# A two-direction recurrence on one core: the inverse's second direction on off-diagonal quarters of the array, work banks in two pairs, the state's update ahead of the transposes

## The reference, cut to what matters

```python
def step(S, inp):
    r_t, w_t, k_t, v_t, kk_t, a_t = inp
    sa = jnp.einsum('bhvk,bhk->bhv', S, -kk_t)
    S = (S * w_t[:, :, None, :] + sa[..., None] * (kk_t * a_t)[:, :, None, :]
         + v_t[..., None] * k_t[:, :, None, :])
    return S, jnp.einsum('bhvk,bhk->bhv', S, r_t)
S, ys = lax.scan(step, S0, xs, reverse=reverse)      # once forward, once in reverse
```

## Time and profile before

| | us |
|---|---|
| median of 3 runs | 2581.54 |
| lowest and highest | 2580.11, 2587.41 |
| the profiled execution | 2585.16 |
| its span in the trace | 2583.6 |
| granted clock of PE, mean | 0.941 of full |

### The profile page before, as it was taken

One profiled execution on the slowest core, in us unless ns is written; L12 is line 12 of the kernel. 1 busy time (PEld: TensorE's weight loads), 2 busy tenths in 40 slices (PEclk: granted clock), 3 DMA queues, 4 the chain that ended last, 5 costly groups with the idle time before them and its releaser, 6 DMA issues. The chain is left out here.

```text
span 2583.6 us, 60917 instructions
## 1 busy us (share of the span) xinstructions
PE 2260.9 (88%) x26659; PEld 1830.6 (71%) x26659; DVE 1146.9 (44%) x1601; ACT 799.4 (31%) x1329; POOL 451.9 (17%) x335
## 2 busy tenths in 40 slices
PE   5899994788888998869799999999696778899998
PEld 3677782677777777757688888888563436688887
DVE  4633322666776667532422222222386652433333
ACT  2223322344334433221522112211433331542231
POOL 0222312644555446300000000000120000000000
PEclk8799896899999999989899999999798989999999
DMA  9566652000000000031122212121110002233332
GB/s 307 173 209 185 192 179 70 23 24 10 30 30 24 30 10 10 10 140 47 49 65 65 72 51 65 57 75 37 44 50 0 0 0 82 73 100 95 98 103 85
DMA packets 261822, 191.73 MB, mean 74 GB/s; under 512 B 11610, under 2 KB 252132, under 8 KB 261092
## 3 DMA queue, kind: packets, MB, share of 16 engines
q1 hardware_dynamic: 261604, 188.45, 24.0%
HBM read 170.60 MB, written 17.83 MB: 73 GB/s over the span
## 5 line engine op out<-in xcount | busy, mean ns | idle before, releaser
L486 DVE TENSOR_TENSOR ffn_lo<-ffn_raw,ffn_hi 128x1024 fp32r<-128x1024 f32 (+1 forms) x120 | 159.8, 1332 | 571.4 <-ACT ffn_hi L481 571.4
L493 PE MATMUL bank<-operand_hi,ffn_hi 128*128 128x512 f32 (+1 forms) x1056 | 378.9, 359 | 24.6 <-DVE operand_lo L455 24.4
L494 PE MATMUL bank<-operand_lo,ffn_hi 128*128 128x512 f32 (+1 forms) x1056 | 378.1, 358 | 0.0
L495 PE MATMUL bank<-operand_hi,ffn_lo 128*128 128x512 f32 (+1 forms) x1056 | 375.0, 355 | 0.0
L481 ACT CAST ffn_hi<-ffn_raw 128x1024 fp32r<-128x1024 f32 (+1 forms) x120 | 136.4, 1137 | 531.3 <-PE bank L495 531.1
L1569 POOL TENSOR_TENSOR lvl<-sc_b,level_mask 128x512 f32<-128x512 f32 x144 | 192.9, 1354 | 320.4 <-PE bank L1158 297.5
L493 PEld LDWEIGHTS bank<-operand_hi,ffn_hi 128*128 128x128 f32 x1056 | 200.4, 190 | 61.8 <-issue 22.4
L495 PEld LDWEIGHTS bank<-operand_hi,ffn_lo 128*128 128x128 f32 x1056 | 200.2, 190 | 29.9
L494 PEld LDWEIGHTS bank<-operand_lo,ffn_hi 128*128 128x128 f32 x1056 | 200.7, 190 | 27.2
L494 PE MATMUL bank<-ffn_g_lo,ffn_hi 128*128 128x512 f32 (+1 forms) x528 | 188.0, 356 | 0.0
L493 PE MATMUL bank<-ffn_g_hi,ffn_hi 128*128 128x512 f32 (+1 forms) x528 | 187.4, 355 | 0.0
(11 more groups left out here) (244 smaller groups left out, 4519.3 us busy)
## 6 DMA issues: line engine op xcount, KB each, us to landing
mod_raw<-in_mod_w SPq DMA_DIRECT2D x96, 512.0 KB, 6.1
ffn_raw<-in_ff_w SPq DMA_DIRECT2D x88, 512.0 KB, 3.9
ffn_raw<-in_ff_w SPq DMA_DIRECT2D x32, 704.0 KB, 4.5
proj_raw<-in_rw_wr SPq DMA_DIRECT2D x8, 512.0 KB, 4.5
proj_raw<-in_rw_wk SPq DMA_DIRECT2D x8, 512.0 KB, 4.6
proj_raw<-in_rw_wv SPq DMA_DIRECT2D x8, 512.0 KB, 4.9
rwkv_out_raw<-in_rw_wo SPq DMA_DIRECT2D x8, 512.0 KB, 4.3
qk_w_raw<-in_at_wq SPq DMA_DIRECT2D x8, 512.0 KB, 3.8
```

The costliest lines, as they stand in the source:

```text
L486: signal(eng, eng.tensor_tensor(self.lo[s][:, 0:k_tiles, :], self.raw[s][:, 0:k_tiles, :], self.hi[s][:, 0:k_tiles, :].bitcast(F32), ALU.s ...
L493: pe.matmul(out, w[0], x[0], start=first, stop=False)
L494: pe.matmul(out, w[0], x[1], start=False, stop=False)
L495: return pe.matmul(out, w[1], x[0], start=False, stop=last)
```

## The change

- T and Y (now L1163, L1173, L1176): the backward direction goes to the two off-diagonal quarters. T writes it to the other half of the partitions in a second bank; Y reads it back. For this Y needs the backward inverses with their halves exchanged, so ACT makes `inverse_swapped` after level 0 and after the additions of levels 1 to 4: two copies of 64x256 each (`swap`, L1498).
- The eight matrices are ordered direction first in `inverse`, `lvl` and `t_sb`; the cut on POOL walks the scores accordingly.
- PSUM: banks 4 to 7 become two pairs of 1024 columns. Every use (scores, turned keys, values, T, Y, side products) takes one of the two pairs in turn. Two-piece side products become one piece of 768 columns, turned keys are copied in one piece of 1024.
- The early parts leave Y and stand in the chain's own blocks: values for y within `u`, for the right-hand side within `rhs`, for the state within `sy`.
- DVE: a new call `flip` holds the transposes. It stands behind `sy`, so the state's update comes after Y's addition and ahead of the transpose.
- `PLACES` has fewer and partly moved entries (the second map moves from place 3 to 4, the third stays at 6, the fourth is at 8, the norm's product at 9).

```diff
@@ schedule
-                y(B, 2, following(0))
+                if B:
+                    y(B, 2)
                 extra(1)
                 if C:
-                    E.sy(C, 0)
+                    E.sy(C, 0, following(0))
+                flip(B, 2)
@@ TensorE
...
+                            elif kind == "score":
+                                pe.wait_ge(masked, 4 * rest[0] + 2 * rest[1] + 2)
...
                     def t(self, G, n):
...
-                        for w in range(2 * GROUP):
-                            for h in range(2):
-                                mm = pe.matmul(bank[half(h), w * CH:w * CH + CH], lvl[G.parity][n % 2][half(h), w, :],
-                                               inv_t[G.parity][half(h), w, :], start=True, stop=True)
+                        for q in range(GROUP):
+                            for e in range(2):
+                                w, out = GROUP * e + q, slice(512 * e + q * CH, 512 * e + q * CH + CH)
+                                for h in range(2):
+                                    mm = pe.matmul(bank[half(h ^ e), out], lvl[G.parity][n % 2][half(h), w, :],
+                                                   inv_t[G.parity][half(h), w, :], start=True, stop=True)
...
+                    def y(self, G, n):
+                        bank = self.work_free("y", G.g, n)
+                        pe.wait_ge(t_copied, self.use.of("t", G.g, n) + 1)
+                        pe.wait_ge(x_swapped, self.use.of("x", G.g, n - 1) + 1)
...
@@ VectorE
-                    def y(self, G, n, _):
+                    def y(self, G, n):
...
-                        if n < LEVELS - 1:
-                            dve.wait_ge(x_added, no + 1)
-                            self.turn_inverse(G)
...
+                    def flip(self, G, n):
+                        dve.wait_ge(x_added, self.use.of("y", G.g, n) + 1)
+                        self.turn_inverse(G)
@@ ScalarE
+                    def swap(self, G, n):
+
+                        for h in range(2):
+                            ins = a.copy(inv_s[G.parity][half(1 - h)], inv[G.third][half(h), GROUP:2 * GROUP, :])
+                        ins.then_inc(x_swapped, 1)
+
+                    def level0(self, G):
+                        act.wait_ge(level0_done, G.g + 1)
+                        self.swap(G, 0)
+
+                    def y(self, G, n):
+                        if n < LEVELS - 1:
+                            act.wait_ge(x_added, self.use.of("y", G.g, n) + 1)
+                            self.swap(G, n)
...
@@ backbone
-        c.bank = [ctx.enter_context(nc.psum_tensor(f"bank{n}", [P, 512], F32)) for n in range(8)]
+        c.bank = [ctx.enter_context(nc.psum_tensor(f"bank{n}", [P, 512], F32)) for n in range(4)]
+        c.pair = [ctx.enter_context(nc.psum_tensor(f"bank_pair{n}", [P, 1024], F32)) for n in range(2)]
+        c.bank += [c.pair[n // 2][:, 512 * (n % 2):512 * (n % 2) + 512] for n in range(4)]
```

More of the change, by code:

```diff
@@ L873, in score @@
             def score(G, i):
-                use.take("bank", "score", G.g, i)
+                use.take("work", "score", G.g, i)
                 E.score(G, i)
             def turn_keys(G):
-                use.take("bank", "keys", G.g), use.take("turn", "keys", G.g)
-                use.take("copy", "b", G.g), use.take("copy", "k", G.g)
+                use.take("work", "keys", G.g), use.take("turn", "keys", G.g)
                 E.turn_keys(G)
@@ L883, in turn_values @@
                 if G.j < 2:
-                    use.take("bank", "values", G.g), use.take("turn", "values", G.g), use.take("copy", "v", G.g)
+                    use.take("work", "values", G.g), use.take("turn", "values", G.g)
                     E.turn_values(G)
@@ L1028, in nothing @@
                 pass
[L1030 to L1035 removed]
+            diag = score = turn_keys = turn_values = level0 = cut = t = y = flip = early = rhs = u = sy = feature = readout = nothing
         with nc.Block() as block:
@@ L1168, in y @@
                             for h in range(2):
-                                mm = pe.matmul(bank[half(h), w * CH:w * CH + CH], t_sb[G.parity][half(h), w, :],
-                                               inv[G.third][half(h), w, :], start=True, stop=True)
-                            if step and w < 6:
-                                self.early_part(*step, w)
-                        mm.then_inc(x_ready, 1)
-                    def early(self, G, q):
-                        self.early_waits(G, q)
-                        for part in range(6):
-                            self.early_part(G, q, part)
@@ L1184, in early_waits, with early, chain_ready @@
+                        mm.then_inc(x_ready, 1)
+                    def early(self, G):
+                        self.chain_ready(G, 0)
+                        for e in range(2):
+                            self.rhs_values(G, 0, e)
+                        for e in range(2):
+                            self.state_values(G, 0, e)
+                    def chain_ready(self, G, q):
+                        need(pe, s_done, G.step(q) - 1)
                         if q == 0:
                             pe.wait_ge(masked, 4 * G.g + 4)
-                            pe.wait_ge(tok_copied, self.use.of("copy", "k", G.g) + 1)
+                            pe.wait_ge(tok_copied, self.use.of("turn", "keys", G.g) + 1)
@@ L1208, in y_values, with rhs_values @@
-                    def y_values(self, G, q, e, done):
+                                pe.wait_ge(tok_copied, self.use.of("turn", "values", G.g) + 1)
+                    def rhs_values(self, G, q, e):
+                        n = G.chunk(q, e)
+                        for h in range(2):
+                            pe.matmul(CHAIN[G.step(q) % 2][half(h), e * CH:e * CH + CH], sc_k[G.third][half(1 - h), q, e, 0, :],
+                                      vtok[G.pair][half(1 - h), n, :], start=(e == 0), stop=False, skip_group_check=True)
@@ new lines, in state_values @@
+                    def state_values(self, G, q, e):
+                        n = G.chunk(q, e)
+                        for h in range(2):
+                            mm = pe.matmul(CHAIN[G.step(q) % 2][half(h), 256 + e * CH:256 + e * CH + CH],
+                                           tok[G.third][half(1 - h), 1, 2 * q + e, :], vtok[G.pair][half(1 - h), n, :],
+                                           start=False, stop=False, skip_group_check=True)
+                        if e == 1:
+                            mm.then_inc(rhs_ready if G.j == q == 0 else early_done, 1)
@@ L1209, in y_values @@
+                    def y_values(self, G, q, e):
                         n = G.chunk(q, e)
@@ L1466, in turn_keys @@
                         need(act, y_ready, GROUP * (G.g - 2))
-                        for i, bank in enumerate((B_BANK, K_BANK)):
-                            a.copy(tok[G.third][:, i], bank[:].rearrange("p (n t) -> p n t", t=CH)).then_inc(tok_copied, 1)
+                        a.copy(tok[G.third][:].rearrange("p i n t -> p (i n t)"), work(self.use, "keys", G.g)[:]).then_inc(tok_copied, 1)
                     def turn_values(self, G):
```

361 lines of the change are left out of this document (178 added, 183 removed).

## The result

The changed kernel takes 2603.09 us (median of 6 runs, 2599.36 to 2617.67), the kernel before 2584.48 in the same comparison: ratio 1.0084, 95% interval [1.0057, 1.0111]. It is slower by 19 us, where 46 us less were forecast.

A forecast was written before the change was run, and what follows sets the result against it. PE was taken as full but not alone on the path, with waits in the chain's loop. Slots -32, last six slots -16, opening slots -3 and clock +5 gave -46 us: 2536 forecast, own range 2505 to 2565, overall 2490 to 2587.

The forecast's parts named there:

- I cost them at nothing: Early parts moved from Y into rhs, u and sy: no cost; 0.23 us per block if their cover failed.
- +1.9 us: Readout slot: the exchange ahead of the square delays step 1's product from 831.7 to 833.6 us.
- 0.74 us each: Exchange on ACT: two copies of 64x256, 120 times, 89 us more ACT time; bounds 0.37 and 1.18 us each.
- rival 2: Whole kernel slower because ACT's queue becomes the chain: 2536 + 71 = 2607 us, chance 0.13.
- I take what is counted above: Two PSUM pairs: only waits already counted, chiefly the fourth map; bounds 0 and 1.2 us per side use.
- Rival 3: The two pairs and their emptying eat the gain: 80 side uses wait 0.5 us each, 2576 to 2580, chance 0.12.
- The state's place: Late step on DVE: the state runs at 3.28 to 3.72 us, since it no longer waits for the transpose.
- late step: Chain step without side work: 5.45 us falls to about 3.9, and a run of such steps settles at about 4.1.
- +5 us: Clock term in the sum: a longer gap in the readout slot adds 0.8 us for six readout slots.
- Rival 4: Lower clock as PE's busy share falls to about 0.75: a quarter of steps slow gives +48, 2584 us; chance 0.08.
- T and Y on four quarters: T and Y blocks on PE each save 0.465 us of issue, 112 us over 240 blocks.

The follow-up runs named there:

- e17: e13 without the exchange and its waits, and with the transposes ahead of the state's update again: 2606.39 us, ratio 1.0083.
- e20: e17 with the early parts back inside Y, between its blocks: 2607.1 us, ratio 1.0084.
- e3: Changed kernel with next-step values moved from rhs to u in a pair's first step and the exchange of levels 2 to 4 behind sy: 2579.19 us, ratio 0.9978.
- e21: e2 with the early parts back inside Y, as before the change: 2588.0 us, ratio 1.0008.
- e1: Changed kernel, but in a pair's first step u and no longer rhs prepares the next step: 2596.22 us, ratio 1.0054.
- e7: Kernel before, with only the new wait of PE for the previous pair's last state in a pair's first step: 2597.31 us, ratio 1.0036.
- e2: Changed kernel with ACT's exchange of levels 2 to 4 behind sy, no longer directly behind u: 2584.79 us, ratio 1.0016.
- e4: Changed kernel with no exchange; Y's second direction reads the inverse as it lies, so that part of the result is wrong: 2582.27 us, ratio 1.0001.
- e18: e3 with the transposes ahead of the state's update on DVE, as before the change: 2587.19 us, ratio 1.0013.
- e6: Kernel before with only the state's update moved ahead of the transposes on DVE: 2584.69 us, ratio 0.999.
- e5: Changed kernel with T and Y on the diagonal quarters again, the exchange made but not used: 2618.56 us, ratio 1.0124.
- e13: e3 with T and Y on the diagonal quarters again: 2597.10 us, ratio 1.0065.

## Why the prediction was wrong

46 us less were forecast and 19 more came, 65 apart. The terms that failed are the two pairs with their pieces (shown, some 20 us), the exchange's place in ACT's queue (shown, 18), the early parts' wait (shown, 7 to 12) and the clock (+5 in the sum; 36 to 60 by an estimate, not shown by a run). In order of the prediction:

- **"I cost them at nothing"** (early parts) is the step that failed first. I looked at their issue, which is indeed free or better (e17 against e20, e3 against e21). I did not look at the wait that they bring: `chain_ready` asks for the previous pair's last state, and in the lone `rhs` it stands ahead of the scores and of everything else on PE. Before, it stood in Y(2), behind them. 7 us in the change (e1), 9 to 12 alone (e7).
- **The readout slot, "+1.9 us"** for the square. The mechanism was right, the exchange ahead of the square behind a late addition. But the addition itself was taken from the old trace at 830.71; it moves with the scores that now come 3 us later. The first step of six readout slots went from 7 to 14 us, where +1.9 was forecast.
- **The exchange, "0.74 us each"**: measured 0.82 a pair of copies. As time on ACT it costs next to nothing (e2 against e4, 2.5 us, within the noise). As a waiting instruction at the head of a queue it costs 18 us (e2). This was rival 2's mechanism, which I gave 0.13 and priced at 71.
- **Two pairs, "I take what is counted above"**: 1.2 us a pair's fourth map and about nothing for the rest; measured about 20 us (e20, e17). Rival 3 named the pairs and gave them 40 us; the new waits for a free pair are 10 us in e20's two rows, and whether the pairs, the pieces or their places cost the rest is not shown. "Not shown by any row" was the warning in my own text.
- **The state's place** was the source of half the gain in the late step, and it holds there (4.16 us; with four quarters but the transposes first, e18, the same steps take 4.9 to 5.9). In the whole kernel it gives 0 (e6) to 8 us (e18).
- **The clock, "+5 us"**: mis-sized. Rival 4 put PE's busy share at 0.75; measured 492/646 = 0.76, which is near for a lucky reason, as both parts were off: 435 busy in 576 us were forecast. PE was busy for longer than forecast in part because the same instructions take longer at half clock (1.55 to 2.92 us above). A fifth of the stretch then ran at half clock, close to rival 4's quarter, for which I had worked out +48. By 0.3 to 0.5 us per us, 119 us more at half clock are an estimate of 36 to 60 us. I treated it as a rival of its own, with 0.08, when it follows from the forecast: whoever takes 47 us of work from PE and none from the waits lowers its share.
- **T and Y on four quarters, 112 us of issue**: the block is as forecast (0.69 for 0.65 us). What it brings on the chip is 10 to 22 us (e5, e13), by medians 15 and 18.

The terms measured one at a time, from pairs of medians: pairs and pieces +23, new wait +7, exchange in the queue +18, exchange elsewhere +2, quarters -10 to -22, early parts' place 0 to -9, state's place -4 to -8 (the 4 is within the noise). Their sum lies between +11 and +36 us for +19 measured: a range this wide fits almost any account, so it confirms no single term, and they don't simply add, as waits hide each other.

Without the wait and with the late exchange (e3), the forecast is still missed by 43 us: some 20 in the pairs and pieces; the rest can, by the estimate above, be the clock (80 us more at half clock than before, 24 to 40 us), which no run shows by itself. Part of it can as well be forecast savings of PE's issue that never were on the path; the runs do not tell the two apart. The clock stood at 0.99 with PE busy for 0.87 of the stretch and at 0.90 with 0.76. The Trainium skill, "TensorE: Matmul & The Clock Gate", Part 1, has the clock follow how busy PE has been; these two rows agree.

## What to carry to other kernels

Work moved to another place in an in-order queue is priced by what it waits for and what stands behind it, not by its length: here one wait, in 7 places, and one pair of 0.4 us copies, behind each addition, cost 24 us together, and moving both by one place gave it back. When a change takes work from the engine whose clock follows its load, put the lower clock into the main sum, and say that its price is an estimate. And a block that gets shorter pays only where the chain ends on it; look for the steps that pay (late ones, 5.45 to 4.16 us) and count them.

## What the runs showed of the hardware

- 32 instructions of 64x64x64 in float32 take 0.69 us on four quarters and 1.10 on two.
- A copy of 64x256 on ACT takes 403 ns, one of 128x256 0.37 us: half the partitions save nothing here (the first reads the tile `inverse`, the other a PSUM bank).
- Granted clock 0.50 shows also while PE is busy without a gap (845 to 848 us, 3.00 of 3.00), behind a gap of 4.55 us.
- At half clock four products of 64x256 columns take 2.92 us in place of 1.55, while DVE, ACT and POOL keep their times. That a step as a whole gets some 0.3 to 0.5 us longer per us at half clock is an estimate from scattered steps.
